# A hybrid decoder layer on one core: zeros on TensorE while the first weights load, both token tiles projected piece by piece, and the last units of attention in another order

## The reference

```python
h = x @ w_in                       # 1024 -> 2240 columns
q_n, kv_n, ... = split(h), rotary on a quarter of each head
o_nsa = gate0*compressed + gate1*selected + gate2*window   # 8 heads of 64
o_dsa = attention over the top 64 keys of a ReLU indexer    # 4 heads
o_mem = attention into 256 memory tokens                    # 4 heads
mix = concat([o_nsa, o_dsa, o_mem]) @ w_out
x = layer_norm(alpha * x + mix, ln1_g, ln1_b)
# PEER: top-16 pairs of sub-keys in each of 8 heads, softmax gates
y[t] = sum_e gate[t,e] * gelu(x[t] . u[e]) * v[e]
x = layer_norm(alpha * x + y, ln2_g, ln2_b)
```

## Time and profile before

| | us |
|---|---|
| median of 3 runs | 1048.59 (1048.1 to 1050.89) |
| the profiled execution | 1048.38 |
| its span, first to last instruction | 1046.3 |
| TensorE busy in the span | 1021.2 (98%) |
| VectorE busy | 741.7 (71%) |
| ScalarE busy | 432.1 (41%) |
| mean granted TensorE clock | 0.989 |

### The profile page before, as it was taken

One profiled execution on the slowest core, in us unless ns is written; L12 is line 12 of the kernel. 1 busy time (PEld: TensorE's weight loads), 2 busy tenths in 40 slices (PEclk: granted clock), 3 DMA queues, 4 the chain that ended last, 5 costly groups with the idle time before them and its releaser, 6 DMA issues.

```text
span 1046.3 us, 17447 instructions
## 1 busy us (share of the span) xinstructions
PE 1021.2 (98%) x6508; PEld 897.1 (86%) x6508; DVE 741.7 (71%) x1797; ACT 432.1 (41%) x763; POOL 106.8 (10%) x210
## 2 busy tenths in 40 slices
PE   7999998999999999999999999999999999999996
PEld 2468874799999999999999999988888888888885
DVE  1166433569889969999999985566666667666667
ACT  1245432123444565555555544443433434334341
POOL 1000000000300043333333310000000000000000
PEclk9999988999999999999999999999999999999998
DMA  9732200385455544444444445657555555565551
GB/s 331 301 140 122 81 21 1 112 300 213 151 183 188 184 163 142 142 142 138 140 139 137 139 152 185 223 184 240 187 197 195 189 198 191 192 199 189 196 181 41
DMA packets 48755, 176.52 MB, mean 169 GB/s; under 512 B 5136, under 2 KB 6176, under 8 KB 47520
## 3 DMA queue, kind: packets, MB, share of 16 engines
q1 hardware_dynamic: 48272, 173.82, 48.1%
q0 software_dynamic: 400, 1.58, 0.5%
HBM read 174.33 MB, written 1.05 MB: 168 GB/s over the span
## 4 chain that ended last, share of the span: by engine, by line
PE 96%; DVE 2%; DMA 1%; ACT 0%; SPq 0%; issue 0%; DVEq 0%
PE ps L464 94%; PE ps L636 1%; DMA arena<-in_w_tok 1%; DVE xs L1662 0%; DVE xs L1656 0%; DVE arena L1650 0%; DVE xs L1647 0%; SPq L358 0%; ACT arena L968 0%; PE ps L676 0%; PE ps L703 0%; PE ps L536 0%; PE ps L525 0%; DVE slab L1355 0%; SPq L359 0%
## 5 line engine op out<-in xcount | busy, mean ns | idle before, releaser
L464 PE MATMUL ps<-x1hl,hi 128*128 128x256 f32 x2216 | 377.7, 285 | 0.0
L464 PEld LDWEIGHTS ps<-x1hl,hi 128*128 128x128 f32 x2216 | 327.3, 192 | 0.0
L464 PE MATMUL ps<-hi,ahl 128*128 128x512 f32 x992 | 265.3, 389 | 0.0
L1099 ACT CAST hi<-slab 128x1024 fp32r<-128x1024 f32 x128 | 135.0, 1055 | 204.8 <-PE ps L464 204.6
L464 PEld LDWEIGHTS ps<-hi,ahl 128*128 128x128 f32 x992 | 186.2, 188 | 38.5
L464 PE MATMUL ps<-x1hl,lo 128*128 128x256 f32 x688 | 194.6, 283 | 0.0
L1612 DVE TENSOR_TENSOR lo<-slab,hi 128x1024 fp32r<-128x1024 f32 x128 | 155.9, 1218 | 0.0
L464 PE MATMUL ps<-lo,ahl 128*128 128x512 f32 x496 | 152.7, 389 | 0.0
L464 PEld LDWEIGHTS ps<-x1hl,lo 128*128 128x128 f32 x688 | 131.7, 191 | 0.0
L1389 DVE TENSOR_TENSOR lo<-slab,hi 128x1024 fp32r<-128x1024 f32 x86 | 106.1, 1233 | 16.3 <-ACT hi L987 16.2
L464 PE MATMUL ps<-arena 128*128 128x128 f32 (+6 forms) x800 | 110.4, 293 | 2.9 <-ACT arena L968 1.6
(11 more groups left out here) (200 smaller groups left out, 825.5 us busy)
## 6 DMA issues: line engine op xcount, KB each, us to landing
slab<-in_pv SPq DMA_DIRECT2D x128, 512.0 KB, 4.2
slab<-in_uT SPq DMA_DIRECT2D x107, 512.0 KB, 3.2
arena<-in_wq SPq DMA_DIRECT2D x32, 512.0 KB, 4.8
ahl_raw<-in_uT SPq DMA_DIRECT2D x21, 512.0 KB, 3.1
arena<-in_w_tok SPq DMA_DIRECT2D x2, 2048.0 KB, 16.8
arena<-in_w_out SPq DMA_DIRECT2D x1, 4096.0 KB, 13.4
arena<-in_w_tok SPq DMA_DIRECT2D x4, 512.0 KB, 8.4
arena<-in_w_tok SPq DMA_DIRECT2D x1, 1792.0 KB, 19.0
```

The source lines that it names most:

```text
L464: return nc.tensor.matmul(o, lhsT, rhs, start=start, stop=stop, skip_group_check=True)
L1099: nc.scalar.copy(hi[:, v_hi_slot(c), :], raw[:, v_slot(c), :]).then_inc(v_hi, 1)
```

## The change

`before` is on the minus side. Four things are done: three matmuls on a tile of zeros are put ahead of the first real one; chunk 0 is multiplied for both tiles as each piece lands; the list of units and what is put between them is rearranged (window units of tile 1 ahead of the memory units of tile 0, four `values` matmuls in each of units 10 to 13, `turn_out(0, 0)` ahead of `turn_out(0, 1)`, other places for the DVE and ACT steps); and the end of the front interleaves `mix(1)` with the transposes, which go to banks 6 and 7.

```diff
-         + [(1, "sel", g, hs) for g in range(2) for hs in PAIRS] + [(1, "win", 0, hs) for hs in PAIRS]
+         + [(1, kind, g, hs) for kind in ("sel", "win") for g in range(2) for hs in PAIRS]
          + [(0, "mem", 0, EVEN), (0, "mem", 0, ODD)]
-         + [(1, "win", 1, hs) for hs in PAIRS]
          + [(1, "dsa", 0, EVEN), (1, "dsa", 0, ODD), (1, "mem", 0, EVEN), (1, "mem", 0, ODD)])
-MEM0 = 12
+MEM0 = 14
-TURNS = ([("u", u) for u in range(15)] + [("o", 0, 1), ("u", 15), ("u", 16), ("o", 0, 0)]
+TURNS = ([("u", u) for u in range(16)] + [("o", 0, 0), ("u", 16), ("o", 0, 1)]
...
+            def project_first():
+                for k in range(KD):
+                    if k % 2 == 0:
+                        pe.wait_ge(l_first[k // 2], 32)
+                    for t in range(T):
+                        last = mm(ps[:, 4 + t, :], xT_sb[:, k, t * P:(t + 1) * P], w_t[:, k, 0:512], k == 0, k == KD - 1)
+                        if k == KD - 1:
+                            last.then_inc(pe_proj, 1)
...
             def turn_x1(t):
                 pe.wait_ge(x1_ready, t + 1)
+                pe.wait_ge(nsa_scaled, 2 * T)
+                pe.wait_ge(pair_scaled, T)
+                pe.wait_ge(pT_saved, nth("x", t, 0))
                 for part in range(2):
-                    pe.wait_ge(pT_saved, nth("x", t, part))
                     for i in range(4):
-                        last = nc.tensor.transpose(ps[:, 2, i * P:(i + 1) * P],
+                        last = nc.tensor.transpose(ps[:, 6 + part, i * P:(i + 1) * P],
...
-            for _ in project(0, DONE[0]):
+            pe.wait_ge(warm_zero, 1)
+            for _ in range(3):
+                mm(ps[:, 6, :], xb[0][:, 0:P], xb[0], True, True)
+            project_first()
+            for _ in project(2, DONE[0]):
                 pass
...
-                if u in (10, 11):
-                    advance(values, KD)
-                if u == 13:
+                if 10 <= u <= 13:
+                    advance(values, 4)
+                if u == 14:
                     cmp_turn(0)
-                if u == 14:
+                if u == 15:
                     cmp_out(0)
+                if u == 16:
                     turn_out(0, 1)
-                if u == 15:
-                    advance(mix0, 4)
-                if u == 16:
-                    advance(mix0, 4)
-                    turn_out(0, 0)
+                    advance(mix0, 6)
                 if u == 17:
                     advance(mix0, 4)
+                if u == 18:
                     cmp_turn(1)
-                if u == 18:
+                    advance(mix0, 3)
+                if u == 19:
                     cmp_out(1)
+                    advance(mix0, 3)
                 outputs(u)
...
+                if u == 15:
+                    turn_out(0, 0)
                 if u == 16:
                     cmp_scores(1)
-                if u == 17:
-                    advance(mix0, 4)
 
             turn_out(1, 0)
+            mix1 = mix(1)
+            advance(mix1, KD)
             turn_out(1, 1)
-            for _ in mix(1):
-                pass
+            advance(mix1, 4)
             turn_x1(0)
-            for j in range(2 * PH):
-                query(j)
-            turn_x1(1)
-            for j in range(2 * PH, 4 * PH):
+            advance(mix1, 4)
+            for j in range(4 * PH):
+                if j == 2 * PH - 2:
+                    turn_x1(1)
                 query(j)
...  (ScalarE)
-                if u == 19:
-                    root(0)
             save_out_turn(1, 0)
             save_out_turn(1, 1)
+            root(0)
             save_x1_turn(0)
             for j in range(4 * PH):
...
-                if j == 2 * PH:
+                if j == 2 * PH - 2:
                     save_x1_turn(1)
...  (VectorE)
+            v.memset(xb[0], 0.0).then_inc(warm_zero, 1)
             dve.wait_ge(l_const, 16)
...
+                if u == 11:
+                    compress_save()
                 if 8 <= u <= 11:
                     index_round(1)
                     index_round(1)
...
                 if u == 13:
+                    weights(1, "win")
+                    add_window(1)
+                if u == 15:
+                    add_compressed(0)
                     weights(0, "mem")
                     scale_pair(0)
```

More of the change, by code:

```diff
@@ L283, in peer_layer_kernel @@
         l_sk, l_ln2 = sem("l_sk"), sem("l_ln2")
+        warm_zero = sem("warm_zero")
         pe_proj, h_saved = sem("pe_proj"), sem("h_saved")
@@ L481, in project @@
                     for k in range(KD):
-                        if i == 0 and k % 2 == 0:
-                            pe.wait_ge(l_first[k // 2], 32)
                         last = mm(ps[:, 4 + i % 2, 0:w], xT_sb[:, k, t * P:(t + 1) * P], w_t[:, k, c0:c0 + w],
@@ L680, in mix @@
             def mix(t):
-                parts = (1, 0) if t == 0 else (0, 1)
+                parts = (0, 1)
                 pe.wait_ge(l_wo, 16)
@@ L968, in save_x1_turn @@
                     nc.scalar.copy(x1T[t][:, 4 * part:4 * part + 4, :],
-                                   ps[:, 2, :].rearrange("p (k n) -> p k n", k=4)).then_inc(pT_saved, 1)
+                                   ps[:, 6 + part, :].rearrange("p (k n) -> p k n", k=4)).then_inc(pT_saved, 1)
             def save_scores(j):
@@ L1025, in _ @@
                     exps(u + 2)
-                if u in (8, 9, 10, 11):
+                if u in (8, 9):
                     save_memory(u - 6)
+                if u in (11, 13):
+                    save_memory(4 + (u == 13))
                 if u == 9:
@@ L1031, in _ @@
                     cmp_exp(0)
-                if u == 13:
+                if u == 14:
                     save_cmp(0)
-                if u == 14:
+                if u == 15:
+                    save_out_turn(0, 0)
+                if u == 16:
                     save_out_turn(0, 1)
-                if u == 16:
-                    save_out_turn(0, 0)
                     cmp_exp(1)
-                if u == 17:
+                if u == 18:
                     save_cmp(1)
-                if u == 19:
-                    root(0)
             save_out_turn(1, 0)
             save_out_turn(1, 1)
+            root(0)
             save_x1_turn(0)
@@ L1454, in _ @@
                     scale_selected(1)
-                if u == 11:
-                    compress_save()
                 if u == 12:
```

## The result

The changed kernel takes **1032.16 us** (median of 4 runs, 1031.99 to 1032.39), the kernel before on the same chip 1048.37 (1048.1 to 1050.89): ratio 0.984, 95% interval 0.9823 to 0.9857. Its profiled execution took 1032.03 us with a span of 1030.0. TensorE waits less, and its clock no longer falls.

A forecast was written before the change was run, and what follows sets the result against it. TensorE, 98% busy over the span, was taken as the bound, with about 24 us in the front not work at full speed. 2.26 + 12.3 + 1.7 = 16.3 us off 1048.38 gave 1032.1; range 1030 to 1037.5.

The forecast's parts named there:

- Term 1: First load: zeros and piecewise matmuls bring the end of chunk 0 from 23.02 to 20.76 us, gain 2.26 us.
- fallback: First load, if zeros did nothing for the clock: two of piece 1's four matmuls slow, gain falls to 1.3 us.
- Term 2: From turn(10) to the first query: 15.5 us of waits and low clock off, 3.2 us put back, net 12.3 us.
- Term 3: At turn_x1(1): 2.60 us with two copies waited for becomes eight transposes in 0.87 us, gain 1.7 us.
- Behind the front: Queries, top-16 and expert blocks follow in the same order and come forward with TensorE, cost 0.
- rival 1: Clock falls in units 14 to 16, 6.9 to 10.3 us at half clock, price 3.5 to 4 us: 1036; chance 0.18.
- 2, waits that only move: DVE or ACT later in units 13 to 15, or x1 late at turn_x1(0), 2 us and more: 1034.5; chance 0.11.
- 3, zeros without effect: At the first load, zeros do not raise the clock or are too late: 1033.1; inside the forecast's 0.65.
- 4: Clock falls in unit 14 and does not rise again before the mix of tile 1: 1060, slower; chance 0.03.
- 5, the gain taken up in the experts: TensorE's gain is taken up by DMA or DVE in the expert blocks: 1047 to 1049; chance 0.03.

The follow-up runs named there:

- a2: Kernel before with chunk 0 multiplied for both tiles piece by piece, without the three zero matmuls: 1049.73 us, ratio 0.9998.
- c1: Changed kernel without the zero matmuls: 1034.98 us.
- e: Changed kernel run again unaltered, on another chip: 1032.38 us, ratio 0.9848 to the kernel before.
- b3: Changed kernel with root(0) back ahead of the copy of turn_out(1, 0) on ACT: 1037.83 us.
- b4: Changed kernel with mix matmuls dealt out again, to stand in the three waits left for ACT's copies: 1029.51 us, ratio 0.9815 to the kernel before.
- d1: Kernel before with only the middle changed (unit order, values four by four, compressed branch, mix(0)); first load, root and tail as before: 1043.5 us, ratio 0.9948.
- b2: Changed kernel with the value matmuls of units 12 and 13 put back into units 10 and 11, eight each: 1042.35 us.
- b1: Kernel before with five idle matmuls added, two in unit 12 and three in unit 13, result unread: 1046.3 us, ratio 0.9975.
- a1: Kernel before with only the first load changed, three zero matmuls and chunk 0 piece by piece: 1045.99 us, ratio 0.9977.
- a3: Kernel before with only the end of the front changed (root behind both copies, mix(1) in three parts, x1 transposes through banks 6 and 7): 1038.63 us, ratio 0.9907.
- a0: Kernel before with the zero matmuls only, first load in the old order: 1049.02 us, ratio 0.9999.
- a4: Kernel before with one line moved, root(0) behind the two copies on ACT: 1043.98 us, ratio 0.9954.

## Why the prediction was right

Forecast 1032.1, measured 1032.16. The two profiled executions differ by 16.35 us; 16.3 was the sum. The mechanisms came as forecast; that the sum is right to 0.1 us is in part luck. Its errors cancel (term 1 gave 0.13 more, term 2 0.36 less, 0.3 came from no term), and it counts from one execution of the kernel before, whose low stretch in units 12 to 14 was 10 us where other executions have 3.5 to 13.5. By its steps:

- **Term 1, 2.26 us: 2.39.** The scores ahead of turn(10) came from 114.27 to 111.88. The zeros ended at 6.1 (forecast about 6.0), the wait for piece 2 is 0.29 us. **Its fallback was wrong:** without a rise from the zeros the prediction left 1.3 us of the term, 1033.1. a2 gained nothing, and c1 took 1034.98. The step that failed is "it rose at 9.7 as before": the moment of the rise isn't fixed. In a2 seven records are slow, up to 12.2 us, and all of them are on the path. In c1 four are, which costs 1.1 us, about what the prediction gave, and the rest of its loss is the late piece. So 1.3 us is what is left in an execution with an early rise and an early piece; the bound from below should have been 0.
- **Term 2, 12.3 us: 11.94** (66.73 us from turn(10) at 113.87 to the first query, before 78.67). Waits taken away and put back: 0.83 + 0.8 + 4.35 + 1.94 were forecast off; the trace lists 7.4 us before and 2.7 after. That leaves 7.2 us for the clock, where 5.0 and 2.3 were forecast. Put back, counted from start to start less the usual pitch: outputs(14) 0.6 for 0.7, turn_out(0, 1) 0.92 for 0.8, the two mix runs 0.93 and 0.84 for 0.86 each: 3.3 for 3.2. cmp_out came without a wait. x1 was ready 0.34 us in time; 0.2 was forecast.
- **Term 3, 1.7 us: 1.73.** `turn_x1(1)` at 208.51, the next query at 209.38: 0.87 for 2.60 in the earlier trace rows.
- **Behind the front, 0:** 0.3 us more is saved than the three terms hold (16.35 against 16.06), and the list of waits has no row for it.

**The rivals.** 1, a fall in units 14 to 16: it didn't come, in none of the six profiled executions that have the values in units 12 and 13 (after, e, c1, b3, b4, d1). It came in b2, in 132 to 143, though the units' order was the new one. So the prediction was right to bank on the clock, but its reason was thin: it argued by which scores stand in the stretch. b2 takes nothing from units 12 and 13 but their run of 256-column matmuls, and the clock falls; b1 gives them idle ones, and it stays. Its price was too low as well: 3.5 to 4 us for a low stretch of 6.9 to 10.3, where b2's lasted 13.7 us and cost 6.7 in the trace. With two waits that rival 1 doesn't have, b2 was 8 us later in the trace and 10 in the median. Rival 1 at b2's price of 6.7 gives 1038.8, beyond the range's 1037.5. 2, waits that only move: they came to 3.3 us, as walked. 3, zeros without effect: excluded, and priced too low in the median (1034.98 for 1033.1). 4 needs a clock that stays low through mix runs; in b3 one run of eight matmuls, 9.3 us long, brought it back. 5, the gain taken up in the experts: it arrived whole.

The prediction weighed the Trainium skill's rule that the full clock does not engage for transposes (TensorE: Matmul & The Clock Gate, Part 4). Units 14 to 16 hold 22 transposes and ran at 1.00 in all those executions; the runs are against the rule as a reason for a fall here. Whether transposes hold the clock less well than other small matmuls, no run tells. The Trainium skill (same page, Part 1) says that activity releases the clock. The zeros agree with it: real records every 0.43 us from 6.21 on.

What stays open: what sets the length of a low stretch. In units 12 to 14 it was about 3.5 us in a1 and a3, 10 in the kernel before, in a0 and in a4, and 13.5 in a2 and b2, and all of these but b2 have the same code in units 10 to 18. For b2 a longer one is plausible, though argued only: between its last values matmul and its first mix matmul lie 24.9 us (124.68 to 149.54), in the kernel before 18.4 (126.81 to 145.25). Nor is it shown how much of each fall is the small matmuls' and how much the short waits' between them.

## What to carry to other kernels

Read the clock column by stretch before the waits: two falls cost 7.2 of the 16.2 us here and are in no list of waits. Spread the large matmuls that fill gaps over the units that have none, rather than stacking them where they are first possible (8 us for one line). Matmuls on zeros during a load pay only if the real work behind them is then ready to use the faster clock; and a copy's wait is covered by two large matmuls that don't need it, wherever they come from.

## What the runs showed of the hardware that was not expected

- How long the array stays at half rate at the start differs from execution to execution. From the first real record to the first at the 0.43 us pitch it is 3.5 us in c1, 5.0 in a3, 6.0 in a2, 6.1 in d1 and 8.7 in b1 (5.90 to 14.59, with a wait of 0.7 between); from the first zero record it is 3.4 us in b4, 3.5 in e, 4.1 in the changed kernel and 5.9 in a0 (7.30). The zeros are worth their place because they start 4.5 us before the weights are there, so that even a late rise is over soon after the first piece.
- Most of the spread of the kernel before comes from the clock. Of its 55 runs, the four with a mean granted clock of 0.992 took 1046.5 to 1046.8 us, the 35 with 0.989 took 1047.9 to 1050.6, and the one with 0.985 took 1054.4. Kernels with its falls: 1046.5 to 1054.4 (before), 1045.7 to 1055.3 (a2). Kernels with neither fall: 1031.99 to 1032.96 over 8 runs (the changed kernel), 1029.48 to 1029.99 over 4 (b4). Even the start differs: in b1's execution the records were slow up to 14.6 us, and its scores ahead of turn(10) are 1.3 us late though nothing was changed up to there.
- The first piece of weights lands anywhere from 5.9 to 7.7 us (TensorE's first real record: 5.90 in b1, 6.74 in d1, 7.73 in c1). In the changed kernel a start at 7.02 instead of 6.21 (e) moved the scores ahead of turn(10) by 0.27 us only.
